# Placing the buffers that matmuls read at multiples of 2048 bytes in a two-block transformer kernel

## What is computed

```python
h = _rms_norm(x, norm_mix[l])
u = h @ w_in[l]
...
y = gates[:, :, 0] * (o_nsa @ proj_nsa[l]) + gates[:, :, 1] * (o_rwkv @ proj_rwkv[l])
x = x + y @ w_out[l]
x = x + _conv_ffn(_rms_norm(x, norm_ffn[l]), ffn_up[l], ffn_conv[l], ffn_down[l])
```

```python
f = swiglu(rmsnorm(x, ffn1_pre_g[l]), ffn1_w_gate[l], ffn1_w_up[l], ffn1_w_down[l])
x = x + 0.5 * rmsnorm(f, ffn1_post_g[l])
y = hybrid_mixer(rmsnorm(x, mix_pre_g[l]), positions, w_in[l], ...)
x = x + rmsnorm(y, mix_post_g[l])
f = swiglu(rmsnorm(x, ffn2_pre_g[l]), ffn2_w_gate[l], ffn2_w_up[l], ffn2_w_down[l])
return x + 0.5 * rmsnorm(f, ffn2_post_g[l])
```

## Time and profile before

| | |
|---|---|
| median of 3 runs | 2446.37 us (2446.28 to 2447.52) |
| span of the profiled execution | 2445.3 us |
| TensorE busy | 2395.1 us, 98% of the span |
| weight loads (PEld) | 1956.1 us, 80% |
| VectorE, ScalarE, GpSimd busy | 1065.3, 935.3 and 1033.9 us |
| mean granted TensorE clock | 0.990 |
| read from HBM | 200.76 MB, mean 84 GB/s with what is written |

### The profile page before, as it was taken

How to read it: one execution, slowest core, us unless ns; L and a number is a source line. 1 busy time by engine, 2 the same in 40 slices (tenths; PEclk the granted TensorE clock), 3 DMA queues, 4 the chain that set the end, 5 groups by cost and what they waited for, 6 DMA issues and landing times.

```text
span 2445.3 us, 38821 instructions
## 1 busy us (share of the span) xinstructions
PE 2395.1 (98%) x13906; PEld 1956.1 (80%) x13906; DVE 1065.3 (44%) x1843; ACT 935.3 (38%) x1278; POOL 1033.9 (42%) x754
## 2 busy tenths in 40 slices
PE   8999998899999999999999999999999999999999
PEld 6878777777888888888888877887888878888886
DVE  4466475455555522222222855763333448222212
ACT  3345432243555522444423322224434624444322
POOL 4222230035455554555544533443343355555554
PEclk9999999999999999999999899999999998999999
DMA  5211110022222233232233222222222222322232
GB/s 158 70 44 44 61 62 4 3 96 98 90 94 96 100 105 101 89 98 98 95 103 105 98 69 72 84 79 69 78 77 84 71 95 69 100 97 94 95 102 95
DMA packets 60732, 204.21 MB, mean 84 GB/s; under 512 B 10940, under 2 KB 11708, under 8 KB 60380
## 3 DMA queue, kind: packets, MB, share of 16 engines
q1 hardware_dynamic: 55152, 196.45, 24.3%
q10 hardware_dynamic: 5488, 6.44, 0.9%
HBM read 200.76 MB, written 2.10 MB: 83 GB/s over the span
## 4 chain that ended last, share of the span: by engine, by line
PE 89%; DVE 8%; issue 2%; ACT 1%; DMA 0%; SPq 0%; DVEq 0%; ACTq 0%
PE psum L400 86%; DVE rope_t L2537 2%; DVE qk_st L2536 1%; PE psum L647 1%; DVE rope_t L2529 1%; DVE qk_st L2539 1%; PE psum L1087 0%; DVE inv L2154 0%; PE psum L473 0%; PE psum L467 0%; ACT dd L1434 0%; DVE tmp L2455 0%; DVE a_t L2095 0%; PE psum L769 0%; DVE zm L1796 0%
## 5 line engine op out<-in xcount | busy, mean ns | idle before, releaser
L373 POOL TENSOR_TENSOR w_lo<-raw,w_hi 128x512 fp32r<-128x512 f32 x732 | 1005.9, 1396 | 1391.0 <-ACT w_hi L1240 1391.0
L400 PE MATMUL psum<-h_hi,w_hi 128*128 128x512 f32 x2128 | 852.9, 401 | 13.2 <-DVE h_lo L1830 10.0
L400 PE MATMUL psum<-h_lo,w_hi 128*128 128x512 f32 x2128 | 835.6, 393 | 0.0
L1240 ACT ACTIVATE w_hi<-raw 128x1024 fp32r<-128x1024 f32 x366 | 385.9, 1055 | 696.7 <-PE psum L400 681.5
L400 PE MATMUL psum<-h_hi,w_lo 128*128 128x512 f32 x2128 | 535.2, 390 | 0.0
L400 PEld LDWEIGHTS psum<-h_hi,w_hi 128*128 128x128 f32 x2128 | 403.9, 190 | 110.4 <-issue 26.0
L400 PEld LDWEIGHTS psum<-h_lo,w_hi 128*128 128x128 f32 x2128 | 403.9, 190 | 84.0 <-issue 3.2
L400 PEld LDWEIGHTS psum<-h_hi,w_lo 128*128 128x128 f32 x2128 | 399.0, 188 | 83.8 <-issue 0.5
L1796 DVE TENSOR_TENSOR tmp<-psum,rst 128x512 f32<-128x512 f32 x100 | 69.1, 691 | 322.4 <-PE psum L400 322.2
L400 PE MATMUL psum<-hid_hi,w_hi 128*128 128x512 f32 x528 | 208.0, 394 | 0.0
L400 PE MATMUL psum<-hid_lo,w_hi 128*128 128x512 f32 x528 | 208.0, 394 | 0.0
(11 more groups left out here) (427 smaller groups left out, 2615.3 us busy)
## 6 DMA issues: line engine op xcount, KB each, us to landing
raw<-in_w SPq DMA_DIRECT2D x366, 512.0 KB, 3.3
x<-in_x SPq DMA_DIRECT2D x4, 512.0 KB, 6.4
x<-in_x ACTq DMA_DIRECT2D x1, 2048.0 KB, 8.9
out_y<-x SPq DMA_DIRECT2D x8, 256.0 KB, 2.3
mask<-in_mask ACTq DMA_DIRECT2D x1, 1536.0 KB
tmp<-in_cmp_w ACTq DMA_DIRECT2D x2, 512.0 KB, 6.0
masks<-in_masks ACTq DMA_DIRECT2D x1, 768.0 KB, 4.8
lora<-in_lora ACTq DMA_DIRECT2D x1, 512.0 KB, 3.5
```

Of the source, the lines that this page charges most:

```text
L373: pool.tensor_tensor(w_lo[:, g.slot, part], raw[:, g.slot, part], w_hi[:, g.slot, part].bitcast(F32), ALU.subtract).then_inc(sem("lo_ready ...
L400: return pe.matmul(out, lhsT, rhs, start=start, stop=stop)
L1240: act.activation(w_hi[:, g.slot], raw[:, g.slot], ACT.Copy).then_inc(sem("hi_ready"), 1)
```

## The change

Only addresses change. The small tables (`par` to `moment`) are taken ahead of the large buffers, and three unused buffers are taken as pads, so that what follows them begins at a multiple of 2048. No instruction is added, removed or moved on any engine, and no shape changes.

```diff
     with ctx:
 
+        par = sb("par", [128, NPAR])
+        ident = sb("ident", [128, 128])
+        blk64 = sb("blk64", [128, 128])
+        idd = sb("idd", [128, 64])
+        sel = sb("sel", [128, 8])
+        stat4 = sb("stat4", [128, 2, TB])
+        spare = sb("spare", [128, 8])
+        moment = sb("moment", [128, 2, TB])
+        sb("page_pad", [128, 304])
         raw = sb("raw", [128, 2, 1024])
...
         tmp = sb("tmp", [128, 8, T])
-        par = sb("par", [128, NPAR])
-        ident = sb("ident", [128, 128])
-        blk64 = sb("blk64", [128, 128])
-        idd = sb("idd", [128, 64])
-        sel = sb("sel", [128, 8])
         rst = sb("rst", [128, T])
-        stat4 = sb("stat4", [128, 2, TB])
-        spare = sb("spare", [128, 8])
-        moment = sb("moment", [128, 2, TB])
...
         ys = ExitStack()
+        sb("y_pad", [128, 456], scope=ys)
         y_hi = sb("y_hi", [128, KD, T], F32R, scope=ys)
...
         par_if = sb("par_if", [4, 2], scope=z2)
+        sb("att_pad", [128, 248], scope=z2)
         att = ExitStack()
```

## The result

| | before | changed |
|---|---|---|
| median | 2446.94 us (4 runs, 2446.28 to 2449.09) | 2431.02 us (4 runs, 2430.03 to 2433.40) |
| ratio | | 0.9932, 95% interval 0.9918 to 0.9946 |
| span of the profiled execution | 2445.3 us | 2429.6 us |

The changed kernel is faster by 0.68%, 15.9 us between the medians. The interval of the ratio stands for a gain of 13 to 20 us; the forecast was a gain of 13.8.

What follows compares the result with a forecast made beforehand. TensorE, busy 2395.1 of 2445.3 us, was taken as the bound, a queue of matmuls. The 13.8 us from hid, y and ah, all other parts 0, gave 2446.4 - 13.8 = 2432.6 us; range 2376 less 2 to 2449 us.

Steps and rivals of the forecast that it cites:

- The main step: Matmuls streaming hid, y, y2 and ah: 2064 go from 233.3 to 226.7 ns each, a gain of 13.8 us.
- the nearest row: For matmuls with hid, y and ah: the 226.7 ns that h has in the trace, taken as their new cost.
- the bounds: For matmuls with hid, y and ah: 233.3 ns as now, gain 0; 213.3 ns, gain 41.3 us.
- `h` unchanged: 6384 matmuls with h, moved with the weights from residue 128 to 0: 0; bounds 85 us less, 42.6 us more.
- `pj_in`: 192 matmuls whose tiles lie at residues 4n and 120 after the change: 0, bounds 1.3 us either way.
- Small matmuls and other engines: Small float32 matmuls and the other engines: 0; on VectorE's chain place might be worth 4 us either way.
- the pair of operations held against each other: Operations on tmp alone (781 ns) and on tmp, hid_hi, hid_lo (797 ns): 2%, possibly from place, 4 us.
- One sign that the prediction had named as a wrong one: Profile after: same matmul spacings, but DVE operations on hid, qk_st or rope_t of another duration.
- The deeper gain: Rival, chance 0.12: h also gains because tiles no longer cross a multiple of 2048; 2376 us, down to 2320 us.
- Nothing moves: Rival, chance 0.20: the 6.7 ns come from the address region, not the residue; 2446 us, give or take 4.
- Slower: Rival, chance 0.10: multiples of 2048 are worse than residue 128 for h; 233.3 ns throughout, costing 42.6 us, 2489 us.

Runs made afterwards that it cites:

- the second comparison: The changed kernel and the kernel before measured again on one chip: 2434.04 us (6 runs) against 2443.85 us (11 runs), ratio 0.9958.
- weights_off: Changed kernel with raw, w_hi and w_lo placed behind tmp, w_hi at residue 64, w_lo at 128, streamed tiles but pj_in's at 0: 2476.28 us, ratio 1.0124.

## Why the prediction was right

**The forecast.** 2432.6 us, measured 2431.02; the gain 13.8 us, measured 15.9, and 9.8 in the second comparison (2434.04 against 2443.85). The pieces of the chain that contain these matmuls account for 13.6. The main step, two speeds of one instruction and 2064 matmuls that change from the one to the other, holds to the last digit in the trace: 3.5 us in each down product, 226.7 ns for `hid`, `y` and `ah`. Taking the nearest row, 226.7 ns, rather than a point between the bounds was right, since these matmuls do exactly what those with `h` do. It did not take the true rule to get there: the change gives these tiles both properties that `h` had, and the one that matters, the distance to the weights, was among them.

**`h` unchanged.** Right, 0: 226.7 ns before and after. The reason given, that the distance to the weights is kept, was the true one of the two that the text named; "both remain multiples of 128" was not needed, as the kernel with everything at residue 64 shows.

**`pj_in`.** Right, 233.3 ns before and 233.1 after.

**Small matmuls and other engines.** Right to take 0. VectorE is busy for 1065.3 and 1065.1 us, and the pair of operations held against each other has 781 and 796 ns after the change, with all its operands at residue 0, where it had 781 and 797, so that its 2% were not a matter of place. One sign that the prediction had named as a wrong one did appear: the operations on `rope_t` and `qk_st` with `rope` went from 1814 to 1773 ns and from 1514 to 1551 ns. They moved against each other, their sum stayed at 79.8 and 79.7 us, and why is not shown.

**The deeper gain.** It did not come: `h` and all others stay at 226.7 ns with tiles that cross no multiple of 2048. The rule of the Trainium skill ("TensorE: Matmul & The Clock Gate", section "Back-to-back issue gap": columns / 2.4 + 2.5 ns, here 215.8 ns) was reached in none of the placements; the lowest mean of a stage was 226.7 ns. The section calls this the isolated gap, without a weight load for each matmul, which the prediction left out. For fp32r tiles of 512 columns with a weight load for each, the measured 226.7 ns stands.

**Nothing moves.** Out by the run that moved `hid` alone by 1344 bytes. The argument that `pj_in`, at steps of 4 bytes, costs as much as `hid` at multiples of 64 looked like evidence against alignment; in fact both missed multiples of 256 bytes from the weights, and most misses cost the same. The Trainium skill ("SBUF — State Buffer", section "SBUF: two separate sides") says that TensorE never waits on anyone. As a rule about other engines, the runs do not contradict that. As a rule that every spacing is alike, which is how the prediction used it, they do: the same matmuls cost 226.7 or 232.8 ns by the place of their weights alone. That the streaming read and the weight read wait for each other is the nearest explanation of a cost that goes by their distance; no view shows such a wait by itself.

**Slower.** The price (233 ns for `h` too) was near the mark as a size: moving the weights by 64 and 128 bytes gave 232.8 ns, and made the kernel 45 us slower than the changed one. But it takes another distance, which this change does not make.

What the prediction did not have is the rule. It said "a multiple of 128, or the residue of the weights" where it is the distance to the weights modulo 256.

## What to carry to other kernels

When TensorE is the bound, take from the timeline the distance between starts of equal matmuls in each stage, and compare stages: a difference of 3% in one instruction with the same shape is worth a look at addresses. The busy share does not show it, and the mean durations mislead: `h_hi` had 401 ns and `hid_hi` 394, though `h` is the faster. For fp32r matmuls with 512 streamed columns and a weight tile each, put the streamed tiles at a multiple of 256 bytes from the weight tiles, by a few dozen bytes of padding; alignment of all buffers to something large does that as a by-product, and only if the weights are included. A part-way measure can lose: the streamed tiles all at multiples of 2048, with the weights 64 bytes off, is 1.2% slower than no alignment at all.

## What the runs showed that was not expected

- Distance 64 modulo 256 costs 2.2 ns over the best, and the other distances measured (16, 32, 96 and from 128 on) cost 5 to 10 ns. The 2.2 ns repeat to 0.1 ns in four kernels. The curve is not symmetric: 192 costs 6.6.
- A weight tile of half the width beside the same stream (134 in place of 188 ns of weight load) made the stream slower, 230.5 against 226.7 ns.
- A stream at distance 0 can need some matmuls at about 230 ns before it runs at 226.7. Right behind matmuls at a dear distance it did, and right behind matmuls at distance 0 it did not (the rows at 1952.06 us above). Behind a break it still does in the changed kernel: from 1509.06 us six starts lie 230.8 ns apart.
- At half clock the matmuls pay nothing over their columns, 427 ns at distance 0. With `w_hi` 64 bytes off it is the same: in weights_off the starts of high matmuls with `h` from 2087.40 to 2090.39 us, at half clock, lie 2.99 / 7 = 427 ns apart. So the price of the distance was seen at the clock of 2.4 GHz alone.
